# The first tile of five weighted products, formed ahead of the stage barrier

## The chip, the core and the metric

One core of a Trainium2 chip runs the whole program in one launch. The metric is the device time of that core in microseconds, and less is better.

## What is computed

The reference is two blocks over 512 latent tokens and 2048 features, in float32. The first is a layer with three branches (a state-space scan with a gated unit, differential attention, attention over a memory of 256 tokens), joined by an output projection. The second is two layers of attention, pooling and Fourier mixing, with 256 context tokens beside the latent ones.

```
def first_block(...):                          # cut to its joints
    y_s = s5_scan(u, ...) ; y_s = gelu(y_s) * sigmoid(gelu(y_s) @ w_glu + b_glu) * silu(g_s)
    y_d = diff_attention(q, k, v, lam, ...) * silu(g_d)
    y_x = memory_attention(q_x, rmsnorm(mem, norm_mem), w_mem_kv) * silu(g_x)
    x = x + rmsnorm(concatenate([y_s, y_d, y_x]) @ w_out, norm_post)
def second_block(...):
    for l in range(2):
        h = rmsnorm_2(x, norm_g[l]) * (1 + scale) + shift
        q, k, v, up, uf, g = split_proj(h @ w_in[l])
        att = latent_attention(q, k, v, kc, vc)
        x = x + gate * merge_branches(att, up, uf, g, ..., w_out[l])
    return rmsnorm_2(x, final_norm_g)
```

## The kernel before

Activations lie feature-major in SBUF: 16 row blocks of 128 features, each 512 latent columns wide, or 768 with the 256 context columns. A weighted product is worked out **tile by tile**: a tile is 128 output features, and needs 16 row blocks k. Both factors are split into a high part, which a copy to the rounded type gives, and a low part, the difference: `h_hi`, `h_lo` for the activations, `w_hi`, `w_lo` for the weights. One row block of one tile is three matmuls, high by high, high by low and low by high. So a tile is 48 matmuls over 512 columns, 48 over 256 for the memory projection, or 96 where both widths are done.

The weights of a tile come by DMA into one of four slots of `raw`. ScalarE (ACT) copies the slot to `w_hi` (L323), VectorE (DVE) forms `w_lo` (L357), and TensorE (PE) multiplies (L398 to L400). `w_hi` and `w_lo` have two places each, so that tile n + 2 can be split only when the products of tile n are done. This is the loop of `linear` (L222). In each turn ACT first splits the weights of tile n and then reads out tile n - 1; DVE does so too.

The program is a row of stages, each an `nc.Block()`. **All engines meet at the end of a block** (the barrier), and none starts on the next before the last has arrived. Queues run in the order that the code is written in; nothing reorders them. The stages that matter here:

- `ssm_and_conditions` (L827), then `linear` for the memory projection (8 tiles of 48 narrow products) with `GluPrepare` (L1141) on ACT and DVE beside it. `GluPrepare` loads 24 arrays at the start and makes the inputs of the gated unit; then `glu` (L1228), 8 tiles of 24 wide products (L1360 to L1362), while GpSimd (POOL) works out the angles of the rotations (L1262 to L1282).
- `middle_attention` (L1613), then `out_projection` (L2119), 16 tiles of 48 wide products.
- `layer_attention` (L1390) of layer 0, then `out_projection`, 16 tiles of 96 products; `layer_attention` of layer 1, then `out_projection`, 16 tiles of 48.

In these stages the first tile's weights were already split by the stage in front (`begun=True`), but its products and the second tile's split came behind the barrier. In the output projections of the two layers the result is added to the residual stream. `reload` (L2165) fetches that in four DMAs of 1.5 MB at the opening of the stage, and `vec_out` (L2133) of tile 0 waits for all four:

```
dve.wait_ge(resid_in.h, resid_in.at(64))            # first tile alone
ins = dve.scalar_tensor_tensor(x, accs[q], g, x, ALU.mult, ALU.add)
```

ACT's part of the same read-out, `act_out` (L2127), squares that sum (L2131) and so waits for it. It stands ahead of the split of the third tile, on ACT and on DVE.

Of the kernel before, what the change touches and what calls it, by code (L numbers as in the profile page):

```python
# [116 lines left out]
def program(nc, cp, const, rope2, cn_sn, cs, invcnt, pos, x_in, mem_in, ctx_in, w_in, w_mem, w_glu,  # L117
            w_out, w_in2, w_out2, ada_w, ssm_b, ssm_c, pool_w, four_w, out):
    ctx = ExitStack()
    with ctx:  # L120
# [47 lines left out]
        def col(name, i=0):  # L168
# [34 lines left out]
            "mask_in", "roped", "norms", "factors", "o_scaled", "turned_back", "d_done", "gate_mult"))  # L203
        first_hi = count("first_hi")
# [16 lines left out]

        def linear(iters, wslot, nk, h0, segs, per_slot=1, store=None, act_out=None, vec_out=None,  # L222
                   stage_at=0, beside=None, keep=None, primed=False,
                   side=None, then=None, ahead=False, begun=False, side_first=False):
# [32 lines left out]
            with nc.Block() as block:  # L257
# [41 lines left out]
                def _(act):  # L299
# [16 lines left out]
                    def body(i):  # L316
                        for j in range(4):
                            n = 4 * i + j
                            if not (begun and first(i) and j == 0):
                                act.wait_ge(raw_full[j].h, raw_full[j].at(16 * (i + 1)))  # L320

                                act.wait_ge(w_used.h, w_used.at((n - 1) * per_slot))
                                act.activation(w_hi[:, j % 2, 0:size], raw[:, j, 0:size], ACT.Copy).then_inc(hi_done.h, 1)  # L323
                            if side and side_first:
                                side.scalar(act, n)
                            if (act_out or store) and not (first(i) and j == 0):
                                read_out(n - 1, (j - 1) % 4)
                            if side and not side_first:
                                side.scalar(act, n)
# [15 lines left out]
                def _(dve):  # L345
# [6 lines left out]
                    def body(i):  # L352
                        for j in range(4):
                            n = 4 * i + j
                            if not (begun and first(i) and j == 0):
# [471 lines left out]
        def ssm_and_conditions(then):  # L827
# [28 lines left out]
            with nc.Block() as block:  # L856
# [90 lines left out]
                def _(act):  # L947
# [51 lines left out]
                    y_copy(chunks - 1)  # L999

                @block.vector
                def _(dve):
# [63 lines left out]
                    conditions(3 * LAYERS - 1)  # L1066
                    dve.wait_ge(st.sem, st.now)
# [3 lines left out]
                def _(pe):  # L1071
# [54 lines left out]
                    turn(3 * LAYERS - 1)  # L1126
            for s, v in ((loaded[0], 32 * chunks), (loaded[1], 16 * chunks), (loaded[2], 16 * chunks), (b_ready, slots // 2),
# [13 lines left out]
        class GluPrepare:  # L1141
# [4 lines left out]
            def tensor(self, pe, slot):  # L1146
                pass
            k0 = math.sqrt(2.0 / math.pi)
# [39 lines left out]
            def vector(self, st, slot):  # L1188
# [17 lines left out]
                if 0 <= c < 8:  # L1206
                    dve.wait_ge(m6.h, m6.at(c + 1))
                    dve.scalar_tensor_tensor(h_lo[:, 8 + c, 0:T], y_at[c], 0.5, h_hi[:, 8 + c, 0:T].bitcast(F32),
                                             ALU.mult, ALU.subtract).then_inc(st.step(), 1)

            def end(self):
                for c in range(8):
                    loaded[c].base += 48
                for m in (m1, m2, m3, m4, m5, m6, tanh_g, silu_done):
                    m.base += 8
# [12 lines left out]
        def glu():  # L1228
# [13 lines left out]
            with nc.Block() as block:  # L1242
# [109 lines left out]
                def _(pe):  # L1352
                    for b in range(8):
# [36 lines left out]
        def layer_attention(l, then):  # L1390
# [27 lines left out]
            with nc.Block() as block:  # L1418
# [81 lines left out]

                @block.gpsimd
# [20 lines left out]
                def _(act):  # L1522
# [44 lines left out]
                    result_high(total // 2 - 1)  # L1567

                @block.vector
                def _(dve):  # L1570
# [33 lines left out]
                    result(total // 2 - 1)  # L1604
                    st.end()
# [7 lines left out]
        def middle_attention(then):  # L1613
# [47 lines left out]
            with nc.Block() as block:  # L1661
# [139 lines left out]

                @block.gpsimd
                def _(pool):
# [22 lines left out]
                    def low_diff(j):  # L1826
                        pool.wait_ge(mixd_hi.h, mixd_hi.at(j + 1))
                        pool.tensor_tensor(h_lo[:, 8 + j, 0:T], gate[j], h_hi[:, 8 + j, 0:T].bitcast(F32), ALU.subtract)

                    def low_mem(pr):  # L1830
# [3 lines left out]
                                           h_hi[:, 12 + j, c0:c0 + CT].bitcast(F32), ALU.subtract)  # L1834
# [12 lines left out]
                def _(act):  # L1847
# [77 lines left out]
                    high_mem(2 * H - 1)  # L1925

                @block.vector
                def _(dve):
# [108 lines left out]
                    result_mem(2 * H - 1)  # L2037
                    st.end()
            for s, v in ((mask_in, 16), (loaded[0], 16 * H), (loaded[1], 16 * H), (loaded[2], 32 * H), (loaded[3], 32), (loaded[4], 32),
# [5 lines left out]
                         (res_done, 2 * H), (res_hi, 2 * H), (first_hi, 1)):  # L2045
# [73 lines left out]
        def out_projection(weights, base, segs, gate_layer, then=None, side=None, begun=False):  # L2119
# [49 lines left out]
            def load_context(sp):  # L2169
                for q in range(4):  # L2170
# [4 lines left out]
                   beside=load_context if gate_layer is None else reload, primed=True, begun=begun, then=then, ahead=then is not None, side=side,  # L2175
# [722 lines left out]
        linear(2, lambda n: row(w_mem, n), KC, 0, [(T, W)], store=lambda n: row(mkv, n), primed=True, side=prep, side_first=True,  # L2898
# [148 lines left out]
```

## Time and profile before

| | |
|---|---|
| median of 3 runs | 2970.73 us (2969.41 to 2974.12) |
| profiled execution | 2971.86 us |
| its span | 2970.1 us |
| granted TensorE clock, mean | 0.981 |
| PE busy | 2818.9 us (95%) |
| DVE, ACT, POOL busy | 1514.0, 990.7, 488.0 us |
| read from and written to HBM | 375.25 MB, 69.86 MB |

The span is that of the profiled execution, and the time beside it holds 1.8 us that lie around it. Busy time is a share of the span; a granted clock of 1.00 is 2.4 GHz, 0.50 is 1.2 GHz. An entry such as `[2.28 <-PEq L1418]` says that the engine sat idle for 2.28 us before this instruction, and what ended it: `PEq` is the sequencer of PE at a barrier.

### The profile page before, as it was taken

What the parts mean: (1) busy time and instruction counts of PE and PEld (TensorE: products, weight loads), DVE (VectorE), ACT (ScalarE), POOL (GpSimd) and SP (SyncE); (2) the same over time, 40 slices, a digit from 0 to 9 for tenths busy, and PEclk for the clock granted to TensorE, in tenths of its full rate; (3) what the DMA queues carried; (4) which work ended last, traced back from release to release, by engine and by line L of the source; (5) the groups of instructions that cost most, each with busy time, mean ns of one, the idle gap of its engine ahead of it and who ended that gap; (6) DMA issues with size and microseconds to landing.
All of it is one profiled execution on the core that took longest, in us unless ns stands there. A gap on an engine that the chain in (4) does not pass through costs nothing. (4 is left out here: it accounts for less than half of the span.)

```text
span 2970.1 us, 36237 instructions
## 1 busy us (share of the span) xinstructions
PE 2818.9 (95%) x14018; PEld 2224.1 (75%) x14018; DVE 1514.0 (51%) x2062; ACT 990.7 (33%) x1717; POOL 488.0 (16%) x597
## 2 busy tenths in 40 slices
PE   7899999999779989999999999999989999989997
PEld 5666666668458868888888877788878877867785
DVE  6587778777663551135523436322253385546334
ACT  4444444445353342112212126311142222226321
POOL 2454444423331040000000002100010000002000
PEclk9999999999889999999999999999999999999998
DMA  5577777774232242233333342322313444441421
GB/s 184 193 293 302 299 277 310 297 291 171 101 102 93 99 156 90 92 130 121 120 105 117 123 156 67 115 92 84 124 46 108 151 165 149 150 171 61 163 100 56
DMA packets 111687, 447.20 MB, mean 151 GB/s; under 512 B 11440, under 2 KB 19760, under 8 KB 76208
## 3 DMA queue, kind: packets, MB, share of 16 engines
q1 hardware_dynamic: 111536, 445.16, 41.2%
q8 instruction: 98, 1.61, 0.2%
q14 instruction: 53, 0.43, 0.0%
HBM read 375.25 MB, written 69.86 MB: 150 GB/s over the span
## 5 line engine op out<-in xcount | busy, mean ns | idle before, releaser
L2780 PE MATMUL ps<-h_hi,w_hi 128*128 128x512 f32 x1600 | 576.9, 361 | 0.0
L2781 PE MATMUL ps<-h_lo,w_hi 128*128 128x512 f32 x1600 | 565.2, 353 | 0.0
L2782 PE MATMUL ps<-h_hi,w_lo 128*128 128x512 f32 x1600 | 561.4, 351 | 0.0
L398 PE MATMUL ps<-h_hi,w_hi 128*128 128x512 f32 (+1 forms) x1152 | 412.0, 358 | 12.1 <-PEq L1418 4.6
L399 PE MATMUL ps<-h_lo,w_hi 128*128 128x512 f32 (+1 forms) x1152 | 411.8, 357 | 0.0
L400 PE MATMUL ps<-h_hi,w_lo 128*128 128x512 f32 (+1 forms) x1152 | 409.8, 356 | 0.0
L2780 PEld LDWEIGHTS ps<-h_hi,w_hi 128*128 128x128 f32 x1600 | 301.9, 189 | 49.8 <-issue 6.2
L2781 PEld LDWEIGHTS ps<-h_lo,w_hi 128*128 128x128 f32 x1600 | 301.6, 189 | 46.6 <-issue 6.2
L2782 PEld LDWEIGHTS ps<-h_hi,w_lo 128*128 128x128 f32 x1600 | 300.7, 188 | 43.6
L2556 DVE TENSOR_TENSOR w_lo<-raw,w_hi 128x2048 fp32r<-128x2048 f32 x64 | 146.4, 2288 | 312.0 <-ACT w_hi L2456 311.9
L398 PEld LDWEIGHTS ps<-h_hi,w_hi 128*128 128x128 f32 x1152 | 219.5, 190 | 46.3 <-issue 10.8
L400 PEld LDWEIGHTS ps<-h_hi,w_lo 128*128 128x128 f32 x1152 | 218.9, 190 | 31.8
L399 PEld LDWEIGHTS ps<-h_lo,w_hi 128*128 128x128 f32 x1152 | 219.4, 190 | 30.5
L2409 ACT ACTIVATE xw<-ps 128x512 f32<-128x512 f32 x88 | 42.1, 517 | 593.5 <-PE ps L2782 552.9
L1505 POOL TENSOR_TENSOR h_lo<-xw,h_hi 128x768 fp32r<-128x768 f32 (+1 forms) x16 | 25.4, 1588 | 1234.8 <-ACT h_hi L1553 1234.8
L1121 PE MATMUL ps<-h_hi,w_hi 128*128 128x512 f32 x512 | 203.9, 398 | 15.4 <-DVE w_lo L1028 8.0
L1123 PE MATMUL ps<-h_hi,w_lo 128*128 128x512 f32 x512 | 200.6, 392 | 0.0
L1122 PE MATMUL ps<-h_lo,w_hi 128*128 128x512 f32 x512 | 200.4, 391 | 0.0
L2131 ACT ACTIVATE wide<-xw 128x512 f32<-128x512 f32 (+3 forms) x48 | 33.8, 703 | 480.2 <-DVE stat L2155 417.3
L2147 DVE SCALAR_TENSOR_TENSOR xw<-ps,mods,xw 128x512 f32 (+3 forms) x48 | 31.8, 662 | 255.4 <-PE ps L400 223.5
L357 DVE TENSOR_TENSOR w_lo<-raw,w_hi 128x2048 fp32r<-128x2048 f32 x52 | 119.8, 2304 | 75.3 <-ACT w_hi L323 75.3
L1121 PEld LDWEIGHTS ps<-h_hi,w_hi 128*128 128x128 f32 x512 | 96.7, 189 | 58.6 <-DVE w_lo L1028 21.7
(394 smaller groups left out, 4716.5 us busy)
## 6 DMA issues: line engine op xcount, KB each, us to landing
raw<-w_in SPq DMA_DIRECT2D x112, 1024.0 KB, 5.2
raw<-ada_w SPq DMA_DIRECT2D x96, 1024.0 KB, 8.6
raw<-w_out SPq DMA_DIRECT2D x48, 1024.0 KB, 5.0
proj<-xw SPq DMA_DIRECT2D x60, 384.0 KB, 2.5
xw<-proj SPq DMA_DIRECT2D x72, 256.0 KB, 3.8
xw<-proj SPq DMA_DIRECT2D x46, 384.0 KB, 3.4
xw<-resid SPq DMA_DIRECT2D x8, 1536.0 KB, 12.3
proj<-wide SPq DMA_DIRECT2D x32, 256.0 KB, 11.0
```

The lines of the kernel that those rows point to most:

```text
L357: dve.tensor_tensor(w_lo[:, j % 2, 0:size], raw[:, j, 0:size], w_hi[:, j % 2, 0:size].bitcast(F32), ALU.subtract).then_inc(lo_done.h, 1)
L398: pe.matmul(a_[q], wh, h_hi[:, h0 + k, lo:hi], start=k == 0, stop=False)
L399: pe.matmul(a_[q], wh, h_lo[:, h0 + k, lo:hi], start=False, stop=False)
L400: ins = pe.matmul(a_[q], wl, h_hi[:, h0 + k, lo:hi], start=False, stop=k == nk - 1)
L1121: pe.matmul(acc, wh, h_hi[:, k, 0:T], start=k == 0, stop=False)
L1122: pe.matmul(acc, wh, h_lo[:, k, 0:T], start=False, stop=False)
L1123: ins = pe.matmul(acc, wl, h_hi[:, k, 0:T], start=False, stop=k == KC - 1)
L2409: act.activation(stage[par][:, a:b], a_, ACT.Copy)
L2556: dve.tensor_tensor(w_lo[:, j % 2, :], raw[:, j, :], w_hi[:, j % 2, :].bitcast(F32), ALU.subtract).then_inc(lo_done.h, 1)
L2780: pe.matmul(a_[q], wh, h_hi[:, k, a:b], start=k == 0, stop=False)
L2781: pe.matmul(a_[q], wh, h_lo[:, k, a:b], start=False, stop=False)
L2782: ins = pe.matmul(a_[q], wl, h_hi[:, k, a:b], start=False, stop=k == KC - 1)
```

## The change

The products of the first tile move from behind the barrier to the end of the stage in front of it, on PE. They are written **row by row**: one row block at a time, each behind a wait for the parts of `h` that it reads. `open_tile` writes the three (or six) matmuls of a row. In the layers' attention the order is the rows of the mixed channels (8 to 15) first, and then the heads. The split of the second tile's weights moves too, to the end of the stage in front, on ACT and DVE. `linear` leaves both out (`opened`). For the gated unit, the rows come from `GluPrepare` while the memory projection ends, and `glu` starts at its second block. Two new counters, `mid_low` and `g_low`, tell PE that low parts are there. Nothing is added to the arithmetic or taken from it. The reload, its place and its wait are as before.

```
+        def open_tile(pe, k, segs, start, stop):
+            wh, wl = w_hi[:, 0, k * P:(k + 1) * P], w_lo[:, 0, k * P:(k + 1) * P]
+            for q, (a, b) in enumerate(segs):
+                acc = bank(q)[:, 0:b - a]
+                pe.matmul(acc, wh, h_hi[:, k, a:b], start=start, stop=False)
+                pe.matmul(acc, wh, h_lo[:, k, a:b], start=False, stop=False)
+                ins = pe.matmul(acc, wl, h_hi[:, k, a:b], start=False, stop=stop)
+            return ins
...
@@ linear: scalar, and vector likewise
-                            if not (begun and first(i) and j == 0):
+                            if not (begun and first(i) and j < (2 if opened else 1)):
@@ linear: tensor
+                            if opened and first(i) and j == 0:
+                                continue
...
+                    if side_first:
+                        side.open_next(pe)
@@ ssm_and_conditions: scalar, vector, tensor
                     y_copy(chunks - 1)
+                    act.wait_ge(raw_full[1].h, raw_full[1].at(16 * (slots + 1)))
+                    act.wait_ge(w_used.h, w_used.at(slots))
+                    act.activation(w_hi[:, 1, :], raw[:, 1, :], ACT.Copy).then_inc(hi_done.h, 1)
...
                     conditions(3 * LAYERS - 1)
+                    dve.wait_ge(hi_done.h, hi_done.at(slots + 2))
+                    dve.tensor_tensor(w_lo[:, 1, :], raw[:, 1, :], w_hi[:, 1, :].bitcast(F32), ALU.subtract).then_inc(lo_done.h, 1)
...
                     turn(3 * LAYERS - 1)
+                    pe.wait_ge(lo_done.h, lo_done.at(slots + 1))
+                    pe.wait_ge(staged.h, staged.at(slots))
+                    for k in range(KC):
+                        ins = open_tile(pe, k, [(T, W)], k == 0, k == KC - 1)
+                    ins.then_inc(w_used.h, 1)
@@ GluPrepare
+            def open_next(self, pe):
+                pe.wait_ge(lo_done.h, lo_done.at(9))
+                pe.wait_ge(staged.h, staged.at(7))
+                for k in range(8):
+                    wh, wl = w_hi[:, 0, k * P:(k + 1) * P], w_lo[:, 0, k * P:(k + 1) * P]
+                    pe.wait_ge(m6.h, m6.at(k + 1))
+                    pe.matmul(bank(0), wh, h_hi[:, 8 + k, 0:T], start=k == 0, stop=False)
+                    pe.matmul(bank(0), wl, h_hi[:, 8 + k, 0:T], start=False, stop=False)
+                    pe.wait_ge(g_low.h, g_low.at(k + 1))
+                    ins = pe.matmul(bank(0), wh, h_lo[:, 8 + k, 0:T], start=False, stop=k == 7)
+                ins.then_inc(w_used.h, 1)
@@ glu: tensor
-                    for b in range(8):
+                    for b in range(1, 8):
@@ layer_attention: tensor (scalar and vector split tile 1 at their ends, as above)
                     weighted(total // 2 - 1)
+                    pe.wait_ge(lo_done.h, lo_done.at(1))
+                    pe.wait_ge(exp_done.h, exp_done.at(total))
+                    order = [(q + HEADS2) % KC for q in range(KC)]
+                    for k in order:
+                        if k == HEADS2:
+                            pe.wait_ge(mixd_lo.h, mixd_lo.at(HEADS2))
+                        if k in (0, HEADS2 - 1):
+                            pe.wait_ge(res_lo.h, res_lo.at(pairs * (HEADS2 - 1) if k == 0 else pairs * HEADS2))
+                        ins = open_tile(pe, k, [(0, T)] if width == T else [(0, T), (T, W)], k == order[0], k == order[-1])
+                    ins.then_inc(w_used.h, 1)
@@ middle_attention: tensor (scalar and vector split tile 1 at their ends, as above)
                     columns(2 * H - 1)
+                    pe.wait_ge(lo_done.h, lo_done.at(1))
+                    pe.wait_ge(exp_done.h, exp_done.at(exps(UNITS - 1)))
+                    for k in range(KC):
+                        if k in (8, 15):
+                            pe.wait_ge(mid_low.h, mid_low.at(10 if k == 8 else 12))
+                        ins = open_tile(pe, k, [(0, T)], k == 0, k == KC - 1)
+                    ins.then_inc(w_used.h, 1)
```

**How the instructions move.** First PE, at the end of the last layer's attention and the opening of the last output projection; before (the two branches are the barrier):

```order
L1484 MATMUL ps<-xw,wide 128x256 x6
L1472 MATMUL ps<-ident_sb,xw 128x128 x6
L1484 MATMUL ps<-xw,wide 128x256 x6
L1418 UNCONDITIONAL_BRANCH
L378 UNCONDITIONAL_BRANCH
L398 MATMUL ps<-h_hi,w_hi 128x512
L399 MATMUL ps<-h_lo,w_hi 128x512
L400 MATMUL ps<-h_hi,w_lo 128x512
```

and in the changed kernel, where 48 such matmuls stand ahead of the branches:

```order
L1525 MATMUL ps<-xw,wide 128x256 x6
L1513 MATMUL ps<-ident_sb,xw 128x128 x6
L1525 MATMUL ps<-xw,wide 128x256 x6
L228 MATMUL ps<-h_hi,w_hi 128x512
L229 MATMUL ps<-h_lo,w_hi 128x512
L230 MATMUL ps<-h_hi,w_lo 128x512
```

The 16 row blocks of tile 0 have moved in front of the barrier; their order among themselves and their number are as before.

Then ACT at the same place. L323 is the split of a tile, tile 1 the first time, L2131 the read-out of a tile; before:

```order
L1543 ACTIVATE xw<-ps 128x6x128
L1549 ACTIVATE h_hi<-xw 128x256 x2
L1418 UNCONDITIONAL_BRANCH
L298 UNCONDITIONAL_BRANCH
L323 ACTIVATE w_hi<-raw 128x2048
L2131 ACTIVATE wide<-xw 128x512
L323 ACTIVATE w_hi<-raw 128x2048
L2131 ACTIVATE wide<-xw 128x512
```

and in the changed kernel, where the same lines are L335 and L2199, and L1621 is the split of tile 1:

```order
L1595 ACTIVATE xw<-ps 128x6x128
L1601 ACTIVATE h_hi<-xw 128x256 x2
L1621 ACTIVATE w_hi<-raw 128x2048
L1459 UNCONDITIONAL_BRANCH
L310 UNCONDITIONAL_BRANCH
L2199 ACTIVATE wide<-xw 128x512
L335 ACTIVATE w_hi<-raw 128x2048
L2199 ACTIVATE wide<-xw 128x512
```

The first instruction behind the barrier is now the read-out of tile 0, and the split of tile 2 stands behind it, as it did.

At the opening of the memory projection ACT stood so (L1175 is the first square of `GluPrepare`, L313 the read-out):

```order
L951 ACTIVATE wide<-ps 128x512
L956 ACTIVATE wide<-ps 128x512
L856 UNCONDITIONAL_BRANCH
L298 UNCONDITIONAL_BRANCH
L323 ACTIVATE w_hi<-raw 128x2048
L1175 ACTIVATE xw<-xw 128x512
L313 ACTIVATE xw<-ps 128x256
L323 ACTIVATE w_hi<-raw 128x2048
```

and in the changed kernel it stands so (L1018 splits tile 1, L1215 is that square):

```order
L967 ACTIVATE wide<-ps 128x512
L972 ACTIVATE wide<-ps 128x512
L1018 ACTIVATE w_hi<-raw 128x2048
L872 UNCONDITIONAL_BRANCH
L310 UNCONDITIONAL_BRANCH
L1215 ACTIVATE xw<-xw 128x512
L325 ACTIVATE xw<-ps 128x256
L335 ACTIVATE w_hi<-raw 128x2048
```

The split of tile 2 is still behind the square of `GluPrepare`, which needs its loads.

## Rows read from the trace of the kernel before

**Rows 1.** The waits of the TensorE; total us, times, longest us.
```profile
PE ps L398 <- PEq L1418: 4.6, 2, 2.3
```

**Rows 2.** Timeline, end of the last attention stage; columns: start us, us, engine, line, operation.
```profile
2764.56 2.83 PE L1484 MATMUL ps<-xw,wide 128*128 128x256 f32 x12 [0.95 <-issue]
...
2768.45 0.72 POOL L1511 TENSOR_TENSOR h_lo<-xw,h_hi 128x256 fp32r<-128x256 f32 x1 [2.88 <-ACT h_hi L1549]
...
2769.55 1.91 ACT L323 ACTIVATE w_hi<-raw 128x2048 fp32r<-128x2048 f32 x1 [1.18 <-PEq L1418]
...
2769.67 0.47 PE L398 MATMUL ps<-h_hi,w_hi 128*128 128x512 f32 x1 [2.28 <-PEq L1418]
```

**Rows 3.** Timeline, opening of the output projection behind it.
```profile
2787.86 0.75 DVE L2147 SCALAR_TENSOR_TENSOR xw<-ps,mods,xw 128x512 f32<-128x512 f32 x1 [14.07 <-DMA xw<-resid]
...
2789.42 1.90 ACT L323 ACTIVATE w_hi<-raw 128x2048 fp32r<-128x2048 f32 x1
...
2791.35 2.29 DVE L357 TENSOR_TENSOR w_lo<-raw,w_hi 128x2048 fp32r<-128x2048 f32 x1 [1.38 <-ACT w_hi L323]
...
2793.70 0.50 PE L398 MATMUL ps<-h_hi,w_hi 128*128 128x512 f32 x1 [0.42 <-DVE w_lo L357]
```

**Rows 4.** Timeline, the first layer's attention end and output projection opening.
```profile
1889.41 4.51 PE L1484 MATMUL ps<-xw,wide 128*128 128x256 f32 x12 [0.95 <-issue]
...
1896.21 0.47 PE L398 MATMUL ps<-h_hi,w_hi 128*128 128x512 f32 x1 [2.28 <-PEq L1418]
...
1915.84 1.27 DVE L2147 SCALAR_TENSOR_TENSOR xw<-ps,mods,xw 128x512 f32<-128x512 f32 x2 [15.52 <-DMA xw<-resid]
...
1920.07 2.29 DVE L357 TENSOR_TENSOR w_lo<-raw,w_hi 128x2048 fp32r<-128x2048 f32 x1 [1.24 <-ACT w_hi L323]
...
1931.43 0.40 PE L398 MATMUL ps<-h_hi,w_hi 128*128 128x512 f32 x1
```

**Rows 5.** Stretches: us, busy us (instructions) of PE, PEld, DVE, ACT, POOL, PEclk, DMA share, GB/s.
```profile
2774.00:2793.30 19.30, 19.28 (x85) 15.59 (x84) 3.29 (x4) 2.44 (x2) 0.00 (x0) 1.00 0.96 381
1900.20:1931.60 31.40, 31.40 (x181) 27.52 (x180) 4.37 (x6) 2.65 (x2) 0.00 (x0) 1.00 0.48 187
708.30:712.40 4.10, 4.08 (x10) 3.24 (x11) 2.26 (x1) 1.81 (x1) 0.43 (x1) 0.50 0.61 199
```

**Rows 6.** Timeline, end of the memory projection, and the gated unit behind it.
```profile
705.51 1.29 DVE L1208 SCALAR_TENSOR_TENSOR h_lo<-xw,h_hi 128x512 fp32r<-128x512 f32 x2
...
708.32 0.77 PE L1360 MATMUL ps<-h_hi,w_hi 128*128 128x512 f32 x1 [5.58 <-PEq L257]
...
748.67 0.78 POOL L1282 TENSOR_SCALAR wide<-wide 128x512 f32<-128x512 f32 x1
...
750.96 0.63 ACT L1310 ACTIVATE wide<-wide 128x512 f32<-128x512 f32 x1
```

**Rows 7.** Timeline, end of the middle attention and the projection behind it.
```profile
878.59 0.72 POOL L1833 TENSOR_TENSOR h_lo<-xw,h_hi 128x256 fp32r<-128x256 f32 x1 [1.07 <-ACT h_hi L1894]
...
879.79 0.76 PE L398 MATMUL ps<-h_hi,w_hi 128*128 128x512 f32 x1 [2.19 <-PEq L1661]
...
892.50 0.69 DVE L2141 COPY xw<-ps 128x512 f32<-128x512 f32 x1 [8.59 <-PE ps L400]
```

**Rows 8.** Timeline, the memory projection's opening.
```profile
652.21 0.36 PE L398 MATMUL ps<-h_hi,w_hi 128*128 128x256 f32 x1 [2.74 <-PEq L856]
...
656.94 0.75 DVE L1193 SCALAR_TENSOR_TENSOR xw<-xw,cv 128x512 f32<-128x512 f32 x1 [7.17 <-DMA xw<-proj]
...
659.95 0.39 PE L398 MATMUL ps<-h_hi,w_hi 128*128 128x256 f32 x1 [1.74 <-DVE w_lo L357]
...
673.24 0.39 ACT L313 ACTIVATE xw<-ps 128x256 f32<-128x256 f32 x1 [1.50 <-PE ps L400]
```

**Rows 9.** DMA view of 2765 to 2800 us; GB/s in 40 slices, then one issue group.
```profile
GB/s 19 0 0 0 0 0 84 147 407 421 411 421 414 400 407 404 397 404 393 411 400 404 400 404 408 445 421 440 403 412 328 0 0 0 169 328 449 262 9 0
...
xw<-resid SPq DMA_DIRECT2D x4, 1536.0 KB, 11.6
```

More of the change, by code:

```diff
@@ L203, in program @@
             "mask_in", "roped", "norms", "factors", "o_scaled", "turned_back", "d_done", "gate_mult"))
+        g_low, mid_low = count("g_low"), count("mid_low")
         first_hi = count("first_hi")
@@ L219, in program @@
         m1, m2, m3, m4, m5, m6 = (count(f"stage{i}") for i in range(1, 7))
+        def open_tile(pe, k, segs, start, stop):
[6 more added lines that the diff above has]
+            return ins
         def linear(iters, wslot, nk, h0, segs, per_slot=1, store=None, act_out=None, vec_out=None,
                    stage_at=0, beside=None, keep=None, primed=False,
-                   side=None, then=None, ahead=False, begun=False, side_first=False):
+                   side=None, then=None, ahead=False, begun=False, opened=False, side_first=False):
             nslot = 4 * iters
@@ L354, in body @@
                             n = 4 * i + j
-                            if not (begun and first(i) and j == 0):
+                            if not (begun and first(i) and j < (2 if opened else 1)):
                                 dve.wait_ge(hi_done.h, hi_done.at(n + 1))
@@ L1208, in vector @@
                     dve.scalar_tensor_tensor(h_lo[:, 8 + c, 0:T], y_at[c], 0.5, h_hi[:, 8 + c, 0:T].bitcast(F32),
-                                             ALU.mult, ALU.subtract).then_inc(st.step(), 1)
+                                             ALU.mult, ALU.subtract).then_inc(g_low.h, 1)
             def end(self):
@@ L1213, in end @@
                     loaded[c].base += 48
-                for m in (m1, m2, m3, m4, m5, m6, tanh_g, silu_done):
+                for m in (m1, m2, m3, m4, m5, m6, tanh_g, silu_done, g_low):
                     m.base += 8
@@ L1567, in _ @@
                     result_high(total // 2 - 1)
+                    act.wait_ge(raw_full[1].h, raw_full[1].at(16))
+                    act.activation(w_hi[:, 1, :], raw[:, 1, :], ACT.Copy).then_inc(hi_done.h, 1)
                 @block.vector
@@ L1604, in _ @@
                     result(total // 2 - 1)
+                    dve.wait_ge(hi_done.h, hi_done.at(2))
+                    dve.tensor_tensor(w_lo[:, 1, :], raw[:, 1, :], w_hi[:, 1, :].bitcast(F32), ALU.subtract).then_inc(lo_done.h, 1)
                     st.end()
@@ L1925, in _ @@
                     high_mem(2 * H - 1)
+                    act.wait_ge(raw_full[1].h, raw_full[1].at(16))
+                    act.activation(w_hi[:, 1, :], raw[:, 1, :], ACT.Copy).then_inc(hi_done.h, 1)
                 @block.vector
@@ L2037, in _ @@
                     result_mem(2 * H - 1)
+                    dve.wait_ge(hi_done.h, hi_done.at(2))
+                    dve.tensor_tensor(w_lo[:, 1, :], raw[:, 1, :], w_hi[:, 1, :].bitcast(F32), ALU.subtract).then_inc(lo_done.h, 1)
                     st.end()
@@ L2174, in out_projection @@
             linear(4, lambda n: row(weights, n + base), KC, 0, segs, act_out=act_out, vec_out=vec_out,
-                   beside=load_context if gate_layer is None else reload, primed=True, begun=begun, then=then, ahead=then is not None, side=side,
+                   beside=load_context if gate_layer is None else reload, primed=True, begun=begun, opened=begun, then=then, ahead=then is not None, side=side,
                    keep=(lambda n: (row(resid, n), xrow(n)(0, W))) if keeps else None)
@@ L2897, in program @@
         prep = GluPrepare()
-        linear(2, lambda n: row(w_mem, n), KC, 0, [(T, W)], store=lambda n: row(mkv, n), primed=True, side=prep, side_first=True,
+        linear(2, lambda n: row(w_mem, n), KC, 0, [(T, W)], store=lambda n: row(mkv, n), primed=True, side=prep, side_first=True, opened=True,
                begun=True, ahead=True, then=lambda n: w_glu[n])
```

6 lines of the change are left out of this document (3 added, 3 removed).

## Prediction

> **What bounds the kernel now.** The page comes first: PE is busy for 95% of the span, so time is gained only where PE stands idle or runs at a low clock. The waits of PE show both output projections of the layers opening with an idle PE [rows 1]. That tells what the change can win; what it can lose is shown by the timeline at each of the five openings. Take the last one. PE ends its attention work at 2767.39 (2764.56 + 2.83), POOL brings the last low part at 2769.17, all engines pass the barrier at 2769.55, and PE multiplies at 2769.67 [rows 2]. So 2.28 us are idle, and the meeting itself takes 0.38 us after the last arrival.
>
> What follows matters more. VectorE (DVE) reads out the first tile only at 2787.86, and what it waited for is the reload of the residual stream, not PE [rows 3]. ScalarE (ACT) and DVE split the third tile's weights behind that read-out: ACT at 2789.42, DVE from 2791.35 to 2793.64. PE starts the third tile at 2793.70, after 0.42 us of waiting. So from the opening of the stage **24.15 us** pass until a third tile can start, whatever PE does, and the first two tiles fill that time now almost exactly. In layer 0 the same chain takes 26.3 us: opening at about 1896.1, reload used at 1915.84, low part at 1922.36. There the first two tiles last until 1931.43, so that 9 us are in hand [rows 4].
>
> **Prices.** In the stretch at full clock 85 products over 512 columns take 19.3 us, 0.227 us each; a tile of 48 is 10.9 us. In the wide projection 181 take 31.4 us, so a tile of 96 is 16.7 us, and one over 256 columns takes 2 x 0.1735 - 0.227 = 0.120. Right behind the 5.58 us of idle PE ahead of the gated unit, the clock was 0.50 for 4.1 us and 10 products passed instead of 18 [rows 5, 6]. A longer idle therefore costs 1.8 us more behind it. No row has a PE idle for 9 or 13 us followed by such products; I take that price and bound it by 0 and 2.
>
> **Last output projection.** The first tile runs from 2767.4 to 2778.3 and drains by 2778.4; the barrier opens at 2778.8. Both splits of the second tile (1.91 and 2.29 us) [rows 2, 3] end by about 2773 beside those products, and the last row's low part is there at 2769.17: both cost nothing. But the stage, and with it the reload, now opens 9.25 us later than at 2769.55. The second tile lasts until 2789.8. The third may start 24.15 us after the opening, at 2802.95: PE is idle for 13.1 us. Against 2793.70 that is **+9.25**, and **+1.8** for the clock. The removed idle wins nothing here, since PE waits for the same chain.
>
> **Output projection of layer 0.** PE ends its attention at 1893.92 [rows 4]. The first tile ends at 1910.6, the barrier opens at 1911.2, that is 15.1 us later. The second tile ends at 1927.9, the low part of the third is there at 1937.45 (1922.36 + 15.1). Before, the third started at 1931.43: **+6.0**, and **+1.8** behind 9.5 us of idle.
>
> **Middle output projection.** No residual stream is added here, so no reload is waited for. PE ended at 877.60 (879.79 - 2.19), POOL at 879.31, and the first tile ran until DVE read it at 892.50, part of it at half clock [rows 7]. Now it starts at 877.6 and ends at 888.7, the stage opens at 889.1, and the second tile starts at 889.2 instead of 892.3: **-3.1**. If the moved products met a half clock inside the stage, 1.8 of it would be lost again.
>
> **Memory projection and gated unit.** Here the narrow first tile (48 x 0.120 = 5.8 us) starts at 649.5, when PE had ended (652.21 - 2.74). With drain and barrier the stage opens at about 655.8 instead of 652.1. The loads of the gated unit's inputs start with it and need 4.8 us (DVE at 656.94) [rows 8]. ACT's square and read-out and the third tile's split by ACT and DVE (1.9 and 2.3) stand behind them, so the third tile starts some 10.8 us after the opening, at 666.6; the second ended at 661.7. The removed wait of 1.74 us at 659.95 comes back as one of 4.9, with the half clock behind it. The third tile ends at 674.1, against 673.2 before: +0.9. From there PE paces as before and ends at 703.6 instead of 702.74 (708.32 - 5.58). The 24 products of the gated unit's first tile follow within the stage: 5.4 us, to 709.2 with the drain, and the barrier at 709.6 [rows 6]. Before it opened at about 708.1, because the last store had to land. DVE's last low part (706.80, now near 707.7) comes before PE reaches its row. So the gated unit starts 1.5 us later, with one tile done. That tile does not help: POOL's angles are ready 41.3 us after the opening (749.45), ACT's sine takes them at 750.96 after 1.3 us for its table, and the last two read-outs queue behind it. With POOL unchanged that point only moves by the 1.5, less the 0.2 that ACT was late: **+1.3**, between -0.2 and +2.5.
>
> **Sum.** 11.05 + 7.8 - 3.1 + 1.3 = **+17.05 us**. Against the profiled execution's 2971.86 that is 2988.9; that execution lies 1.1 above the median of the runs, 2970.73, so the median becomes **2987.8**.
>
> **The reload's rate.** Its price is the largest in the sum, so it is bounded apart. It is four times 1536 KB, 6.29 MB. Once rolling, the engines move 393 to 445 GB/s [rows 9]; at 421 from the first byte it would take 14.9 us instead of 18.3 and 19.7. Nothing in the change speeds it, and the weights' loads are issued behind it, so I take the times as measured [rows 3, 4]. The Trainium skill (DMA: Bandwidth & Descriptors, "Where 436 GB/s comes from") says that transfers between HBM and SBUF are held to about 358 GB/s by the memory side, with 435 as the fabric's ceiling; an estimate by the first is 17.6 us, by the second 14.5, which would put the sum near +8. The trace does not agree with the first: its slices pass 400.
>
> **Rivals.**
> - **The reload lands in time (faster).** If the read-out of the first tile were held by PE and not by the reload, both layers would gain as the middle does. The second tiles would end at 1927.9 and 2789.8 instead of 1931.4 and 2793.7: -3.5 and -3.9, with -3.1 and +1.3 together -9.2, so 2961.5. It decides where the reload lands within some 10 us (layer 0) and 5 us (last) of the opening. That asks for over 600 GB/s, against 445 at most [rows 9], and both rows name the reload. For it speaks only that releasers are inferred. 0.04.
> - **The reload lands sooner.** 14.9 us in both: -4.8 and -3.4, so 2979.6. 0.08.
> - **Half clock in the moved products.** PE is busy only in part at the ends of the attention stages, and within its last 4.51 us in layer 0 twelve small products took as long as at a low clock (2.83 in the last layer) [rows 2, 4]. Then each stage opens 1.8 later, three times: +5.4, so 2993.2. 0.14.
> - **The change does not do what it says.** The rows are guarded by counters; if PE started only when the last low part is there, the three wide openings would come 1.7 to 1.8 later: +5.3, so 2993.1. Against it: the first waits are on flags set long before. 0.04.
> - A third tile without any price of the clock, together with a somewhat sooner reload, would end near 2975: 0.03.
>
> **Numbers.** The forecast as worked out has 0.67, with 2983 to 2992 as its own range (the clock's price between 0 and 2, the memory part between -0.2 and +2.5). The full range takes in the sooner reload and the half clock: 2979 to 2995. About 0.2% (5.9 us) is what a measurement of this kernel can tell from no change. Slower by more has 0.93: all but the first rival and the last line; within it 0.03, faster 0.04.
>
> **What would show it.** In the changed profile: the barrier of the last projection near 9 us later relative to the attention's end, with no 2.28 idle ahead of the first product; DVE's first read-out still 18.3 us (layer 0: 19.7) behind the opening; PE idle for 13 and 9.5 us ahead of the third tile, released by DVE's `w_lo`, and a PEclk of 0.50 behind both. In the middle projection no such idle. In the memory projection one near 5 us. If the reload lands within 11 us of the opening, or the third tile's split comes ahead of the first read-out, the forecast is wrong, and it would be wrong in sign.

## The result, and the profile after

| | before | after |
|---|---|---|
| median of 5 runs each, side by side | 2972.55 us (2969.41 to 2977.05) | 2988.72 us (2985.88 to 2997.5) |
| profiled execution, its span | 2971.86, 2970.1 us | 2997.5, 2995.7 us |
| granted TensorE clock, mean | 0.981 | 0.976 |
| PE, DVE, ACT, POOL busy | 2818.9, 1514.0, 990.7, 488.0 us | 2823.7, 1513.2, 989.9, 491.2 us |

The change is **slower by 0.56%**: ratio 1.0056 with an interval of 1.0043 to 1.0069; the medians differ by 16.2 us. The forecast was a median of 2987.8 against one of 2970.73, or +17.05. The profiled execution of after is the longest of its five; 7.2 us of its excess lie in the state-space stage, which the change leaves alone (see the table below). So it is read stage by stage and never by its span.

The waits of PE in the changed kernel; columns: engine and line, what it waited for, total us, times, longest us.

```profile
PE ps L412 <- DVE w_lo L369: 26.9, 3, 12.9
```

Of the waits at the two barriers of the layers [rows 1], 4.6 us together, 0.47 and 0.50 us are left. In their place stand three waits for the low part of the **third** tile's weights, 26.9 us in all: 12.91 in the last layer, 9.05 in layer 0, 4.94 in the memory projection. (The moved rows of a tile keep their number, but in the two layers not their order: before, they ran from 0 to 15; now rows 8 to 15 come first, as the loop over `order` says.) The timeline shows each wait. First the last output projection (start us, us, engine, line, operation, idle ahead of it):

```profile
2778.43 2.83 PE L1525 MATMUL ps<-xw,wide 128*128 128x256 f32 x12 [0.95 <-issue]
2780.91 0.58 PE L228 MATMUL ps<-h_hi,w_hi 128*128 128x512 f32 x1
...
2792.66 0.47 PE L412 MATMUL ps<-h_hi,w_hi 128*128 128x512 f32 x1 [0.50 <-PEq L1459]
...
2810.86 0.75 DVE L2215 SCALAR_TENSOR_TENSOR xw<-ps,mods,xw 128x512 f32<-128x512 f32 x1 [24.49 <-DMA xw<-resid]
...
2812.42 1.89 ACT L335 ACTIVATE w_hi<-raw 128x2048 fp32r<-128x2048 f32 x1
...
2814.35 2.29 DVE L369 TENSOR_TENSOR w_lo<-raw,w_hi 128x2048 fp32r<-128x2048 f32 x1 [1.37 <-ACT w_hi L335]
...
2816.69 0.79 PE L412 MATMUL ps<-h_hi,w_hi 128*128 128x512 f32 x1 [12.91 <-DVE w_lo L369]
```

The attention's own products end at 2781.26 (2778.43 + 2.83), tile 0 follows without an idle, and the barrier costs 0.50 us. PE's first product behind the barrier comes 11.4 us behind the attention's end instead of 2.28 [rows 2]. DVE has the reload 18.20 us behind that product (before 18.19 [rows 2, 3]), and the third tile starts 24.03 us behind it (before 24.03). From the attention's end to the third tile it is 35.43 us instead of 26.31. Layer 0 shows the same:

```profile
1894.77 3.69 PE L1525 MATMUL ps<-xw,wide 128*128 128x256 f32 x9
...
1915.73 0.47 PE L412 MATMUL ps<-h_hi,w_hi 128*128 128x512 f32 x1 [0.47 <-PEq L1459]
...
1935.24 1.27 DVE L2215 SCALAR_TENSOR_TENSOR xw<-ps,mods,xw 128x512 f32<-128x512 f32 x2 [31.67 <-DMA xw<-resid]
...
1941.80 0.80 PE L412 MATMUL ps<-h_hi,w_hi 128*128 128x512 f32 x1 [9.05 <-DVE w_lo L369]
```

Here it is 43.3 us (1941.80 - 1898.46) instead of 37.5 [rows 4]. The middle projection has no reload, and there the change wins:

```profile
885.24 0.58 PE L228 MATMUL ps<-h_hi,w_hi 128*128 128x512 f32 x1
...
896.83 0.69 DVE L2209 COPY xw<-ps 128x512 f32<-128x512 f32 x1 [6.20 <-PEq L1717]
...
896.98 0.47 PE L412 MATMUL ps<-h_hi,w_hi 128*128 128x512 f32 x1 [0.47 <-PEq L1717]
```

Tile 0 starts inside the stage and its read-out comes at once behind the barrier, where DVE had waited 8.59 us for PE [rows 7].

Stretches of the changed kernel (us; busy us and instructions of PE, PEld, DVE, ACT, POOL; PEclk; DMA share; GB/s):

```profile
673.90:677.00 3.10, 3.10 (x14) 3.10 (x15) 2.82 (x5) 3.10 (x6) 0.00 (x0) 0.50 1.06 399
677.00:680.00 3.00, 3.00 (x19) 3.00 (x18) 3.00 (x3) 1.61 (x4) 0.00 (x0) 0.60 1.10 410
...
1905.00:1912.00 7.00, 7.00 (x42) 6.13 (x42) 0.00 (x0) 0.00 (x0) 0.00 (x0) 1.00 0.00 0
...
1941.80:1945.50 3.70, 3.70 (x11) 3.12 (x12) 2.21 (x4) 2.30 (x2) 0.00 (x0) 0.50 0.49 144
...
2816.70:2819.50 2.80, 2.80 (x7) 2.22 (x8) 1.45 (x3) 1.93 (x2) 0.00 (x0) 0.50 0.57 149
2819.60:2822.00 2.40, 2.40 (x12) 1.96 (x11) 1.96 (x1) 0.40 (x1) 0.00 (x0) 1.00 0.59 246
```

Inside the stages the moved products run at 1.00: in layer 0 as shown, in the last layer from 2781.3 to 2792, in the middle from 885.2 to 896. Behind both long idles of the layers the clock is 0.50 (1.2 GHz) for some 3 to 4 us. Behind the 4.94 us of the memory projection it is 0.50 and then 0.60 on average, for some 6 us together (the first two lines).

Last, the memory projection and the gated unit:

```profile
662.93 0.35 PE L412 MATMUL ps<-h_hi,w_hi 128*128 128x256 f32 x1 [0.50 <-PEq L872]
...
667.99 0.75 DVE L1233 SCALAR_TENSOR_TENSOR xw<-xw,cv 128x512 f32<-128x512 f32 x1 [7.12 <-DMA xw<-proj]
...
682.33 0.38 ACT L325 ACTIVATE xw<-ps 128x256 f32<-128x256 f32 x1 [3.73 <-PE ps L414]
...
717.72 0.47 PE L1401 MATMUL ps<-h_hi,w_hi 128*128 128x512 f32 x1 [0.63 <-PEq L269]
...
751.60 1.28 ACT L1350 ACT_TABLE_LOAD   x1
757.67 0.63 ACT L1350 ACTIVATE wide<-wide 128x512 f32<-128x512 f32 x1 [4.79 <-POOL wide L1322]
```

The loads of `GluPrepare` land 5.1 us behind the opening, and PE then waits 4.94 us for the third tile at 673.86. ACT reads that tile out at 682.33. The 5.58 us ahead of the gated unit [rows 6] are now 0.63. In the gated unit ACT loads its table and still has 4.79 us to wait for POOL; before, it came to the table only when POOL was done (its last angle at 749.45, the sine at 750.96 [rows 6]).

**All profiles, stretch by stretch.** Each number is the distance between two instructions, in us: `mem` from the last transposes of the state-space stage to the opening of the gated unit, `glu` from there to the middle attention, `midproj` from the last products of the middle attention to the first root on ACT behind the projection, `proj0` the output projection of layer 0 with the end of its attention, `projL` the last one to the final norm. `ssm` is the start of the program up to `mem`.

```
kernel                                ssm   mem   glu midproj proj0 projL
before                              649.2  58.9  54.9  182.9  279.5 181.3
after                               656.4  61.0  52.3  179.7  287.1 191.8
e10_change_again (after, again)     647.6  62.0  52.2  180.8  287.0 191.9
e1_layers_undone                    651.1  60.9  52.2  179.6  279.5 181.4
e2_quarter_wait                     648.6  62.0  52.1  179.7  276.1 178.6
e3_split_first                      645.9  61.6  52.2  179.6  282.8 187.2
e4_quarter_before                   648.6  56.9  54.7  182.9  279.3 179.0
e5_middle_alone                     646.8  57.3  55.1  179.6  279.5 181.3
e6_extra_load                       649.8  58.4  54.9  183.0  279.4 187.7
e7_quarter_split_all                646.7  60.5  52.2  179.7  276.1 177.2
e8_quarter_mem_undone               650.2  59.5  54.6  179.7  275.9 178.7
e9_quarter_glu_undone               651.8  60.3  54.5  179.7  276.0 178.7
```

### The profile page after: what moved, and what is told of

Same layout as the page of the kernel before. It is cut to its first block and busy times, and to the rows that moved or that the text cites. A ratio compares the mean times of both kernels' runs of the same rounds, so it can differ in the third digit from the quotient of the medians.

```text
span 2995.7 us, 36236 instructions
## 1 busy us (share of the span) xinstructions
PE 2823.7 (94%) x14018; PEld 2227.5 (74%) x14018; DVE 1513.2 (51%) x2062; ACT 989.9 (33%) x1717; POOL 491.2 (16%) x597
## 3 DMA queue, kind: packets, MB, share of 16 engines
q1 hardware_dynamic: 111536, 445.16, 40.8%
## 5 line engine op out<-in xcount | busy, mean ns | idle before, releaser
L412 PE MATMUL ps<-h_hi,w_hi 128*128 128x512 f32 (+1 forms) x1072 | 384.3, 358 | 28.9 <-DVE w_lo L369 26.9
L413 PE MATMUL ps<-h_lo,w_hi 128*128 128x512 f32 (+1 forms) x1072 | 383.6, 358 | 0.0
L414 PE MATMUL ps<-h_hi,w_lo 128*128 128x512 f32 (+1 forms) x1072 | 381.8, 356 | 0.0
L2848 PEld LDWEIGHTS ps<-h_hi,w_hi 128*128 128x128 f32 x1600 | 301.9, 189 | 49.7 <-issue 6.2
L2849 PEld LDWEIGHTS ps<-h_lo,w_hi 128*128 128x128 f32 x1600 | 301.6, 189 | 46.7 <-issue 6.2
L2850 PEld LDWEIGHTS ps<-h_hi,w_lo 128*128 128x128 f32 x1600 | 300.7, 188 | 43.7
L2624 DVE TENSOR_TENSOR w_lo<-raw,w_hi 128x2048 fp32r<-128x2048 f32 x64 | 146.4, 2288 | 310.6 <-ACT w_hi L2524 310.5
L412 PEld LDWEIGHTS ps<-h_hi,w_hi 128*128 128x128 f32 x1072 | 204.5, 191 | 60.7 <-DVE w_lo L369 27.7
L414 PEld LDWEIGHTS ps<-h_hi,w_lo 128*128 128x128 f32 x1072 | 203.8, 190 | 30.0
L413 PEld LDWEIGHTS ps<-h_lo,w_hi 128*128 128x128 f32 x1072 | 204.4, 191 | 28.4
L1142 PE MATMUL ps<-h_hi,w_hi 128*128 128x512 f32 x512 | 205.1, 401 | 18.7 <-ACT wide L967 11.4
L2199 ACT ACTIVATE wide<-xw 128x512 f32<-128x512 f32 (+3 forms) x48 | 33.7, 703 | 499.1 <-DVE stat L2223 436.2
L1142 PEld LDWEIGHTS ps<-h_hi,w_hi 128*128 128x128 f32 x512 | 97.6, 191 | 62.6 <-issue 24.7
L369 DVE TENSOR_TENSOR w_lo<-raw,w_hi 128x2048 fp32r<-128x2048 f32 x48 | 110.7, 2306 | 63.7 <-ACT w_hi L335 63.7
```

The costliest lines, as they stand in the source:

```text
L412: pe.matmul(a_[q], wh, h_hi[:, h0 + k, lo:hi], start=k == 0, stop=False)
L413: pe.matmul(a_[q], wh, h_lo[:, h0 + k, lo:hi], start=False, stop=False)
L414: ins = pe.matmul(a_[q], wl, h_hi[:, h0 + k, lo:hi], start=False, stop=k == nk - 1)
L1142: pe.matmul(acc, wh, h_hi[:, k, 0:T], start=k == 0, stop=False)
L2624: dve.tensor_tensor(w_lo[:, j % 2, :], raw[:, j, :], w_hi[:, j % 2, :].bitcast(F32), ALU.subtract).then_inc(lo_done.h, 1)
L2848: pe.matmul(a_[q], wh, h_hi[:, k, a:b], start=k == 0, stop=False)
```

## The experiments

The theory is that the third tile is gated by the reload, 24 to 26 us behind the opening of the stage, and that the change only moves the opening back. The rivals are a cost of the moved products themselves, a cost of the low clock, and the order of the split behind the read-out. Kernels of one group of runs are compared with the same runs of the kernel before.

### Which part of the change costs the time

**The layers' part taken out**: the products of tile 0 and the split of tile 1 go back behind the barrier, in the two layers alone.

```
@@ layer_attention, tensor (scalar and vector likewise)
-                    for k in order:
...
-                        ins = open_tile(pe, k, ...)
...
@@ out_projection
-  opened=begun
+  opened=begun and gate_layer is None
```

> The changed kernel with the part in the two layers' attention and output projections undone. Gate theory (the third tile waits for the reload's chain from the opening of the stage): all of the loss goes, 18.8 us, and the time is 3.1 us below the kernel before, give or take 1.5 for the memory part. If the loss came from the memory projection or from a disturbed clock all over the program instead, it stays above the kernel before by more than 5 us.

Measured: 2969.26 us against 2970.52, ratio 0.9997 (0.9986 to 1.0008). `proj0` and `projL` are back at 279.5 and 181.4. So the whole loss lies in these two stages: 7.6 + 10.5 = 18.1 us by the table. The 3.1 us below the kernel before that were expected are inside the interval (4.2 us below to 2.4 above); the medians show 1.3.

**The middle projection alone**: the memory projection's and the gated unit's parts are taken out as well.

```
...
@@ memory projection
-  side_first=True, opened=True
+  side_first=True
@@ linear: tensor
-                        side.open_next(pe)
@@ glu: tensor
-                    for b in range(1, 8):
+                    for b in range(8):
```

> The kernel before with the change in the middle attention and its output projection alone. Gate theory: no reload is waited for there, so the time behind the attention falls by 3.1 us (2.2 of idle and the low clock behind it, less the barrier) and the program by as much. If the moved products ran at half clock inside the stage: 1.3 us. In the trace the span from the end of the attention's last product to the last tile's copy shortens by 3.1.

Measured: 2967.86 against 2971.93, ratio 0.9988 (0.998 to 0.9997); `midproj` 179.6, that is -3.3. The gain of the middle stands by itself. The interval of the ratio also holds a gain of 1 us or 6.

### Is it the reload

**The first read-out waits for a quarter.** Tile 0 is added to the first row block, and the reload comes in four DMAs of four row blocks each. The first gets a semaphore of its own; the read-out of the third tile waits for the others.

```
+        resid_rest = count("resid_rest")
-                    dve.wait_ge(resid_in.h, resid_in.at(64))
+                if gate_layer is not None and isinstance(n, int) and n == 0:
+                    dve.wait_ge(resid_in.h, resid_in.at(16))
+                if gate_layer is not None and isinstance(n, int) and n == 2:
+                    dve.wait_ge(resid_rest.h, resid_rest.at(48))
-                    ... .then_inc(resid_in.h, 16)
+                    ... .then_inc((resid_rest if q else resid_in).h, 16)
...
```

> The changed kernel, where the read-out of the first tile waits for the first quarter of the reload alone (its own counter), and that of the third tile for the rest. Gate theory: the first quarter lands some 6 us behind the opening, the stalls of 13 and 9.5 us go with the low clock behind them, and both layers gain as the middle does: 9 us below the kernel before, 26 below the changed one. Rival (the loss is from the products inside the attention stages or from the clock, not from the reload): within 3 us of the changed kernel.

Measured: 2961.79 against 2970.52, ratio 0.9974 (0.9964 to 0.9984). **It beats both kernels.** Its timeline at the last opening:

```profile
2771.38 0.47 PE L413 MATMUL ps<-h_hi,w_hi 128*128 128x512 f32 x1 [0.47 <-PEq L1460]
...
2777.73 0.75 DVE L2218 SCALAR_TENSOR_TENSOR xw<-ps,mods,xw 128x512 f32<-128x512 f32 x1 [12.63 <-DMA xw<-resid]
...
2783.57 0.50 PE L413 MATMUL ps<-h_hi,w_hi 128*128 128x512 f32 x1 [1.03 <-DVE w_lo L370]
```

The first quarter is there 6.35 us behind the opening instead of 18.2, and PE's idle of 12.91 us has become 1.03. `proj0` and `projL` fall by 11.0 and 13.2 against after. The chain from reload to split is the gate, as named.

**The same wait in the kernel before**, with nothing moved.

> The kernel before with the wait for the first quarter alone. Gate theory: before, the two first tiles filled the reload's time, so only the 0.42 us of waiting ahead of the last projection's third tile goes: within 1 us of the kernel before. If the reload had cost the kernel before more than its trace shows: 5 us or more below it.

Measured: 2970.11, ratio 0.9998 (0.9989 to 1.0008). By the runs the quarter wins nothing unless the products are moved, because there the first two tiles cover the chain (0.42 us of waiting were left [rows 3]). Its profile shows `projL` 2.3 us shorter all the same. The clock behind this opening was full there (see the last section), so the third tile started 21.9 us behind it (2790.98 - 2769.11), where the whole wait would have held it until 24.0. How often that happens is open; the interval of the runs holds a gain of 3.3 us and a loss of 2.4. Either edit alone gives no gain that the runs resolve, or a loss, and the two together 8.7 us.

**A longer reload in the kernel before**: one more DMA of 1.5 MB, within HBM, goes ahead of it and is waited for.

```
+        spare = dram("spare", [4, P, W])
-                    dve.wait_ge(resid_in.h, resid_in.at(64))
+                    dve.wait_ge(resid_in.h, resid_in.at(80))
+                sp.dma_start(spare, resid[0:4]).then_inc(resid_in.h, 16)
...
```

> The kernel before with one more DMA of 1.5 MB, from HBM to HBM, ahead of the four of the reload, and the first read-out waits for it too; its data is used nowhere. It delays the first read-out by some 4 to 8 us in both layers. Gate theory: the last projection, which has no slack, gets longer by that and the low clock (6 to 10 us), and that of layer 0, with 9 us in hand, by nothing (0 to 1). If PE's first two tiles were what bound the opening: no change in either.

Measured: 2975.7 against 2971.93, ratio 1.0017 (1.0008 to 1.0025). In layer 0 the read-out comes later and costs nothing (279.4); in the last layer it comes 23.1 us behind the opening and costs 6.4:

```profile
2792.61 0.75 DVE L2148 SCALAR_TENSOR_TENSOR xw<-ps,mods,xw 128x512 f32<-128x512 f32 x1 [18.99 <-DMA xw<-resid]
...
2798.44 0.80 PE L399 MATMUL ps<-h_hi,w_hi 128*128 128x512 f32 x1 [5.30 <-DVE w_lo L358]
```

So in the last layer nothing was in hand, and in layer 0 more than the 5.4 us by which the read-out came later, as the prediction had read from rows 3 and 4. No product is moved here.

### The order of the split, and the accumulators

**The third tile's split ahead of the first read-out**, on ACT and DVE, where no `GluPrepare` stands beside.

```
+                            early = opened and not side
+                            if early and first(i) and j == 0:
+                                act.wait_ge(raw_full[2].h, raw_full[2].at(16))
+                                act.wait_ge(w_used.h, w_used.at(1))
+                                act.activation(w_hi[:, 0, 0:size], raw[:, 2, 0:size], ACT.Copy).then_inc(hi_done.h, 1)
...
```

> The changed kernel with the split of the third tile ahead of the first tile's read-out, on ACT and DVE, in the output projections; the reload and its wait are untouched. Gate theory: the third tile then waits only for its accumulator, which the first read-out frees 19.1 us behind the opening (last) and 21.0 (layer 0), so PE's idle falls from 12.9 to 8 us and from 9.5 to 4.2: 10 us below the changed kernel, 6 above the one before. If the split itself were late for another reason: no change.

Measured: 2978.1 against 2970.52, ratio 1.0022 (1.0013 to 1.0032), that is 7.6 us above the kernel before where after lay 16.2 above it: 8.6 us better, and 8.9 by the table. PE's idle at the last opening has another name and 5 us less:

```profile
2795.59 0.75 DVE L2225 SCALAR_TENSOR_TENSOR xw<-ps,mods,xw 128x512 f32<-128x512 f32 x1 [14.08 <-DMA xw<-resid]
...
2796.48 0.76 PE L422 MATMUL ps<-h_hi,w_hi 128*128 128x512 f32 x1 [7.94 <-DVE xw L2225]
```

Once the weights are ready, PE waits for the read-out itself: the third tile goes into the accumulator of the first. Order alone doesn't cure it; the reload gates twice, through the split and through the accumulator. More accumulators were not tried.

**Quarter wait and early split together**, the memory projection's split too.

```
-                            early = opened and not side
+                            early = opened and True
```

> The changed kernel with both the wait for the first quarter of the reload and the third tile's split ahead of the first read-out, now in the memory projection too, where it goes ahead of the square that waits for the gated unit's inputs. The 4.9 us of idle PE and the low clock behind it in the memory projection should go. If PE paces that stage to its end: 4 to 6 us below the run with the quarter wait alone in the time to the gated unit's opening. If the inputs' loads and the work on ACT and DVE pace it: less than 1.

Measured: 2961.06 against 2971.93, ratio 0.9971 (0.9959 to 0.9982), not to be told from the quarter wait alone. In the layers no wait above 0.5 us is left for PE. In the memory projection the one wait of 4.94 us became three, of 1.3, 2.5 and 1.5, and ACT's next split met its load (waits of ACT from 655 to 680):

```profile
ACT w_hi L337 <- DMA raw<-w_mem: 4.7, 1, 4.7
```

`mem` is 60.5 against 60.9 to 62.0 in the five others that keep the old order with both parts: some 1 us, where 4 to 6 had been expected if PE paced this stage and less than 1 if loads, ACT and DVE did. So the second holds, about: each of the three waits is for a split or a read-out of these two engines. **The idle that was to go has stayed**, 5.3 us in three pieces.

### The memory projection and the gated unit

The quarter wait stays in these two. First both parts are undone, by the edit of the middle alone at the memory projection and the gated unit:

> The run with the quarter wait, with the change in the memory projection and the gated unit undone. It gives the price of that part. The prediction's +1.3 would make this run 1.3 us faster than the run with the quarter wait; if the table load that now lies in a wait pays for the later opening, it is the same within 1 or slower by 0.5.

Measured: 2962.49 against 2971.93, ratio 0.9967 (0.9954 to 0.9979). Then the gated unit's part alone:

```
-                        side.open_next(pe)
-                    for b in range(1, 8):
+                    for b in range(8):
```

> The run with the quarter wait, with the gated unit's first tile back behind the barrier (the memory projection's first tile stays in the stage in front). If POOL's angles pace the gated unit, as the traces say, its stage lasts about 54.8 us instead of 52.1, the memory projection's about 1 to 2 us less than 62.0, and the program's time stays within 1.5 us of the run with the quarter wait. If PE paced it, the stage would last 5 us longer and the program with it.

Measured: 2965.01 against 2969.91, ratio 0.9985 (0.9974 to 0.9995). Both intervals overlap that of the quarter wait (0.9964 to 0.9984), so what these parts are worth isn't resolved. The time of this run was expected within 1.5 us of the quarter wait's; by the medians it is 3.8 us worse (4.9 us below the kernel before instead of 8.7), with intervals of some 3 us to either side. By the table, the sum of `mem` and `glu` is 114.1 with both, 114.1 with neither and 114.8 with the memory part alone. The stages themselves came as expected, 54.5 us for the gated unit and 60.3 for the memory projection.

**The change once more**, for its profile:

> The changed kernel once more, for a second profile. The stage of the state-space scan, which the change leaves alone, took 7.2 us longer in its first profile; if that is the scatter of its many loads, it is back within 3 us of 649.2 here, while the projections of the two layers keep 287.1 and 191.8 us within 1 us. If the change causes it, the scan's stage is at 656 again.

Measured: 2989.68 against 2969.91, ratio 1.006 (1.0045 to 1.0074), span 2986.9. `ssm` is 647.6 this time, so the 7.2 us of the first profile are scatter of a stage that nothing changed. `proj0` and `projL` repeat within 0.1.

## Why the prediction was right

- **What bounds it.** Right: both reloads land as far behind the opening as before (18.20 against 18.19 us; 19.51 against 19.6), and the third tile 24.03 and 26.1 us behind it. The quarter wait removes the loss, the extra load brings one of its kind without the change. This is shown.
- **Last output projection.** Forecast +9.25 and +1.8; measured +9.12 to the start of the third tile (35.43 - 26.31), +10.5 in `projL`, which leaves 1.4 behind it for the clock.
- **Layer 0.** Forecast +6.0 and +1.8; measured +5.8 (43.3 - 37.5) and +7.6 in `proj0`, which leaves 1.8 for the clock. The stage opened 17.3 us behind the attention's end, as worked out (17.3).
- **Middle.** Forecast -3.1, measured -3.2, -2.1 and -3.3 in three profiles.
- **Memory projection and gated unit.** Here two terms were mis-sized, and the errors cancel. The prediction had +1.5 for the opening of the gated unit and -0.2 behind it, with the words "That tile does not help". Over five profiles with both parts (after, e1, e2, e3, e10) `mem` is 61.5 on average and `glu` 52.2; over the five with neither (before, e4, e5, e6, e8) 58.2 and 54.8. So it is +3.3 and -2.6, together **+0.7** against +1.3, while the sums within one group spread over 2.5. That this part of the sum came near is luck.
  - *The tile did help*, in two ways: ACT came to its table 4.8 us before POOL was done, so that 1.5 us of table and delay vanish; and POOL's last angle was ready 39.9 to 40.0 us behind the opening instead of 40.8 to 41.4. With this tile alone put back (e9) both are as before: the table from 753.36 to 754.64, behind POOL's end at 753.15, and 40.8 us. Why POOL is 1.1 us sooner is open.
  - *In `mem`* the opening came 3.5 us later and the wait at the third tile was 4.94 us against 4.9, as forecast. What was too small is the third tile behind it: its read-out on ACT comes 26.2 us behind the last transposes on average in the five with both parts (in after 682.33) and 23.9 in the five with neither (in before 673.24 [rows 8]), so +2.4 where the forecast had +0.9. The prediction let the low clock pass in some 4 us, as ahead of the gated unit [rows 5]; here it lasts some 6, over 33 narrow products. From the end of the memory projection's products to the opening it is 0.6 us more, as forecast.
- **The reload's rate.** Right to take it as measured. With 421 GB/s from the first byte on the median would have been 2979.6; it was 2988.72. The estimate by the two bounds of the Trainium skill (DMA: Bandwidth & Descriptors, "Where 436 GB/s comes from") had put the sum near +8 with the faster one. The trace of after has slices of 382 to 463 GB/s in this reload, and still 18.2 us from the opening to the read-out, so neither bound gives its length. The landings do: in the last layer of after the first quarter lands 6.5 us behind its issue and the others 3.9 us apart, 402 GB/s.
- **Rivals.** The half clock in the moved products fell: 1.00 in all three wide stages. A third tile without a price of the clock fell by the 0.50 behind both idles. "The change does not do what it says" fell too: PE is at its products at once behind the attention. The fast rival, the reload in time, fell by the idles; what it described is what the quarter wait brings about: 2961.8, against the 2961.5 worked out for it.

Sum by the table, after minus before: 7.6 + 10.5 - 3.2 - 0.5 = +14.4 us, with the second profile 7.5 + 10.6 - 2.1 + 0.4 = +16.4. The medians differ by 16.2 and 19.8. The stretches that the table leaves out (the attentions and the input projections) scatter by up to 3 us each.

## What to carry to other kernels

Work that is moved ahead of a barrier also moves the barrier back, and with it every load that is issued behind it: before moving, measure from the opening of the stage to the first work that such a load releases, and compare with what is left to cover it. A wait for the whole of a transfer of which the first user needs a quarter can be free for as long as enough work stands beside it and cost 13 us once that is gone; split the semaphore together with the move. And an engine that "only" gets ahead elsewhere may hide a fixed cost, such as a table load, in a wait that it now has.

## What was not expected of the hardware

**The clock behind a short idle is not the same in each profile.** In the kernel before, 2.28 us of idle PE stand ahead of the last output projection, and then, in a stretch of 2.8 us:

```profile
2769.70:2772.50 2.80, 2.80 (x9) 2.21 (x10) 1.00 (x1) 1.76 (x1) 0.00 (x0) 0.66 0.63 144
```

In the kernel before with the quarter wait, behind the same 2.28 us and ahead of the same products:

```profile
2769.20:2772.00 2.80, 2.80 (x13) 2.31 (x14) 1.06 (x1) 1.71 (x1) 0.00 (x0) 1.00 0.62 161
```

Nine products pass in the one and 13 in the other. The two kernels with nothing moved in the layers and the old wait (e1, e5) have 0.68 and 0.64 there over their first 3 us, and the extra load 0.74. Ahead of layer 0, behind the same 2.28 us of idle, all five have the low clock, 0.58 to 0.62 over the first 2.8 us, the one with the quarter wait too; first the kernel before, then that one:

```profile
1896.20:1900.00 3.80, 3.79 (x13) 3.32 (x14) 1.96 (x1) 1.80 (x1) 0.00 (x0) 0.58 0.62 198
...
1893.30:1897.10 3.80, 3.79 (x13) 3.30 (x14) 1.96 (x1) 1.81 (x1) 0.00 (x0) 0.59 0.75 213
```

What decides it is open. Behind idles of 4 us and more at these openings (4.08 and 7.94 in e3, 5.30 with the extra load, 9 and 12.9 in after and its repetition) the clock was 0.50 each time.

In the kernel before, the low clock at the last opening costs nothing by itself: the first two tiles still end 0.42 us ahead of the reload's chain, and behind that short wait the clock is full:

```profile
2793.00:2796.00 3.00, 2.58 (x12) 1.93 (x11) 2.15 (x4) 1.43 (x2) 0.00 (x0) 1.00 0.36 85
```

So the 1.4 us of the last layer are the price of 0.50 against a full clock, behind the third tile's start. They are less than the 1.8 of the prediction, as the low clock passed in some 3 us: 7 products in 2.8 us instead of 12.3 at 0.227, 1.2 us. In layer 0 it is 11 products in 3.7 us instead of 21 at 0.1735, 1.8 us.

**The state-space stage scatters** between 645.9 and 656.4 us over these profiles. The work up to its last transposes is the same in all of them, and the 10.5 us are more than half the effect that was looked for. Two spans of single profiles would have told 25.6 us of loss where the runs tell 16.
